# Two blocks of a transformer on one core: norms by token, loads and dots in another order, rotation on VectorE

## What is computed

```
x = first_block(x, ...)
    h = rms_norm(x, norm1_g);  proj = h @ w_in
    ya = rglru_group(...)      # y = gelu(gate) * scan;  rms_norm over 256 channels
    yb = fox_group(...)        # softmax attention, 8 heads of 64; rms_norm over 512
    yc = rwkv7_group(...)      # o = (o - mean) * rsqrt(var + GN_EPS) per head of 64,
                               # ... * ln_g + ln_b, plus a bonus, times g
    x = x + concat(ya, yb, yc) @ w_out
    x = x + hier_moe(rms_norm(x, norm2_g), ...)
return second_block(x, c, positions, ...)
    for l in range(2):
        mod = silu(c) @ w_ada[l] + b_ada[l]      # 6 x 1024 numbers per layer
        h = rms_norm(x, norm1) * (1 + sc1) + sh1;  proj = h @ w_in[l]
        # retention (q and k rotated by the position), spatial gating, pooling,
        # branch and output products, then a feed-forward of width 4096
```

## Time and profile before

| | |
|---|---|
| median of 3 runs (lowest to highest) | 2919.86 us (2915.3 to 2921.07) |
| the profiled execution: time, span | 2918.53 us, 2916.7 us |
| mean granted TensorE clock | 0.957 |
| busy: PE, DVE, ACT, POOL | 2737.2, 1510.6, 1115.2, 904.5 us |
| instructions | 34325 |

### The profile page before, as it was taken

One profiled execution on the slowest core, in us unless ns is written; L12 is line 12 of the kernel. 1 busy time (PEld: TensorE's weight loads), 2 busy tenths in 40 slices (PEclk: granted clock), 3 DMA queues, 4 the chain that ended last, 5 costly groups with the idle time before them and its releaser, 6 DMA issues.

```text
span 2916.7 us, 34325 instructions
## 1 busy us (share of the span) xinstructions
PE 2737.2 (94%) x13246; PEld 2262.8 (78%) x13246; DVE 1510.6 (52%) x1661; ACT 1115.2 (38%) x1283; POOL 904.5 (31%) x200
## 2 busy tenths in 40 slices
PE   6999887999989999997989999899999989899997
PEld 4787565988769898886868888688988867788886
DVE  6755566599943420344246766733212351466666
ACT  3423363577732443234332332324342343333222
POOL 2211002000023244343434444232343434344443
PEclk8999688799999999998999999899999999999999
DMA  7110017299812122222234444321222222244443
GB/s 274 58 44 23 30 44 295 110 365 366 313 69 76 55 97 100 87 101 94 87 120 162 186 165 152 106 87 58 90 92 92 96 94 87 107 155 179 169 152 130
DMA packets 65321, 376.66 MB, mean 129 GB/s; under 512 B 7729, under 2 KB 8753, under 8 KB 29873
## 3 DMA queue, kind: packets, MB, share of 16 engines
q1 hardware_dynamic: 63040, 368.58, 34.5%
q10 hardware_dynamic: 2160, 6.42, 0.6%
HBM read 372.86 MB, written 2.10 MB: 129 GB/s over the span
## 4 chain that ended last, share of the span: by engine, by line
PE 75%; DVE 4%; issue 3%; POOL 1%; ACT 1%; ACTq 0%; DVEq 0%; POOLq 0%
PE pd L240 18%; PE pd L241 18%; PE pd L242 18%; PE pd L260 2%; PE pd L261 2%; PE pd L259 2%; PE pd L1765 2%; PE pd L1763 2%; PE pd L1764 2%; POOL sb_w_lo L218 1%; DVE sb_ada_held L369 1%; PE pd L1790 1%; PE pd L1792 1%; PE pd L1791 1%; PE pd L1721 1%
## 5 line engine op out<-in xcount | busy, mean ns | idle before, releaser
L218 POOL TENSOR_TENSOR sb_w_lo<-sb_raw,sb_w_hi 128x2048 fp32r<-128x2048 f32 x189 | 890.8, 4714 | 1818.0 <-ACT sb_w_hi L209 1818.0
L240 PE MATMUL pd<-sb_h_hi,sb_w_hi 128*128 128x512 f32 x1696 | 676.1, 399 | 53.3 <-DVE sb_h_lo L337 25.6
L241 PE MATMUL pd<-sb_h_lo,sb_w_hi 128*128 128x512 f32 x1696 | 666.2, 393 | 0.0
L242 PE MATMUL pd<-sb_h_hi,sb_w_lo 128*128 128x512 f32 x1696 | 665.2, 392 | 0.0
L209 ACT CAST sb_w_hi<-sb_raw 128x2048 fp32r<-128x2048 f32 x189 | 361.3, 1912 | 316.6 <-PE pd L242 314.5
L240 PEld LDWEIGHTS pd<-sb_h_hi,sb_w_hi 128*128 128x128 f32 x1696 | 322.3, 190 | 132.2 <-DVE sb_h_lo L337 29.7
L240 PE MATMUL pd<-sb_y_hi,sb_w_hi 128*128 128x512 f32 x960 | 377.0, 393 | 20.9 <-issue 17.1
L241 PE MATMUL pd<-sb_y_lo,sb_w_hi 128*128 128x512 f32 x960 | 376.3, 392 | 0.0
L242 PE MATMUL pd<-sb_y_hi,sb_w_lo 128*128 128x512 f32 x960 | 376.0, 392 | 0.0
L241 PEld LDWEIGHTS pd<-sb_h_lo,sb_w_hi 128*128 128x128 f32 x1696 | 322.4, 190 | 67.8 <-issue 2.2
L242 PEld LDWEIGHTS pd<-sb_h_hi,sb_w_lo 128*128 128x128 f32 x1696 | 322.1, 190 | 67.8
(11 more groups left out here) (504 smaller groups left out, 3927.8 us busy)
## 6 DMA issues: line engine op xcount, KB each, us to landing
sb_raw<-in_slabs SPq DMA_DIRECT2D x189, 1024.0 KB, 4.8
sb_V<-in_ada SPq DMA_DIRECT2D x64, 512.0 KB, 6.1
sb_V<-in_moe SPq DMA_DIRECT2D x28, 1024.0 KB, 7.0
sb_QK<-in_moe SPq DMA_DIRECT2D x28, 1024.0 KB, 7.1
sb_raw<-in_moe SPq DMA_DIRECT2D x28, 1024.0 KB, 7.1
sb_QK<-in_ada SPq DMA_DIRECT2D x32, 512.0 KB, 6.5
sb_ada_held<-in_ada SPq DMA_DIRECT2D x30, 512.0 KB, 5.4
sb_M<-in_ada SPq DMA_DIRECT2D x12, 512.0 KB, 15.2
```

The lines of the kernel that those rows point to most:

```text
L218: pool.tensor_tensor(w_lo[j][:], raw[j][:], w_hi[j][:].bitcast(F32), ALU.subtract).then_inc(w_lo_ready[j], 1)
L240: pe.matmul(out, w_hi[j][:, cols], hi[:, k], start=(k == 0), stop=False)
L241: pe.matmul(out, w_hi[j][:, cols], lo[:, k], start=False, stop=False)
L242: last = pe.matmul(out, w_lo[j][:, cols], hi[:, k], start=False, stop=(k == KT - 1))
```

## The change

Four parts. (1) At the start: ScalarE loads the table of the root first and applies Silu to c only behind the cast of slab 1; slab 1 is loaded right behind slab 0; the six dots ahead of the first reciprocal are gone, so that the start has twelve instead of eighteen. (2) Attention: the sums of the two norms are made by token. The tile is the stationary operand and one or two columns of ones the moving one, which gives 4 + 16 columns with the tokens on the partitions; root and reciprocal act on these 128 x 20 numbers, and products of a broadcast column with the identity spread them again over the channels. This stage has twenty dots, one behind each of the units 5 to 24; three blocks of queries are turned at the end instead of two. Some banks of PSUM are given out otherwise, so that `pd[3]` is free earlier, and unit 0 waits for all eight normalised tiles. (3) w_out: 6, 6 and 4 dots. (4) Rotation: VectorE multiplies each half of the tile by the sine and writes it to the other half, in two instructions of 64 partitions; the sine has the other sign, and the swap matmuls go.

The diff, cut to its core and moved left by eight columns; the small hunks left out only rename or number banks and semaphores:

```diff
@@ -55,8 +55,8 @@
 PAIRS = LAYERS_AT + LAYERS * LAYER_PAIRS
 ADA_COLS = 48
 ADA_RING = 6
-ADA_BEFORE, ADA_FIRST, ADA_FOX, ADA_HELD = 6, 18, 10, 4
-ADA_LATE = (7, 8, 5)
+ADA_FIRST, ADA_FOX, ADA_HELD = 12, 20, 4
+ADA_LATE = (6, 6, 4)

 CH = 64
...
@@ -496,15 +495,15 @@
         sp.dma_start(xT[:, 2 * n:2 * n + 2], t["x"][:, 2 * n:2 * n + 2]).then_inc(x_loaded[n], 16)
     sp.dma_start(ones[:], t["ones"]).then_inc(vec_loaded, 16)
     sp.dma_start(vec[:, 0:V1_COLS], t["vec1"]).then_inc(vec_loaded, 16)
-    sp.dma_start(raw[0][:], t["slabs"][0]).then_inc(raw_loaded[0], 16)
+    for j in range(2):
+        sp.dma_start(raw[j][:], t["slabs"][j]).then_inc(raw_loaded[j], 16)
     sp.dma_start(c_row_first, t["c_row"].partition_broadcast(P)).then_inc(c_row_first_loaded, 16)
-    for n in range(ADA_BEFORE):
+    for n in range(6):
         sp.dma_start(ada_first[n], t["ada"][n]).then_inc(ada_first_loaded[n // 3], 16)
-    sp.dma_start(raw[1][:], t["slabs"][1]).then_inc(raw_loaded[1], 16)
     sp.dma_start(c1[:], t["c1"]).then_inc(c_loaded, 16)
     sp.dma_start(blk[:], t["blk"]).then_inc(c_loaded, 16)
     sp.dma_start(ident[:], t["ident"]).then_inc(c_loaded, 16)
-    for n in range(ADA_BEFORE, ADA_FIRST):
+    for n in range(6, ADA_FIRST):
         sp.dma_start(ada_first[n], t["ada"][n]).then_inc(ada_first_loaded[n // 3], 16)
     for m in range(1, 3):
...
@@ -769,20 +768,38 @@
     qk_spreads(6)
     qk_spreads(7)

-    def lru_means():
-        pe.wait_ge(qk_norm, 8)
+    def token_sums():
+        pe.wait_ge(lru_sq, 2)
+        pe.wait_ge(ln_sq, 2)
         for j in range(2):
-            pe.wait_ge(lru_sq, j + 1)
-            last = pe.matmul(pd[3][:], ones[:], lru_sqr[:, j], start=(j == 0), stop=(j == 1))
+            for b in range(TB):
+                pe.matmul(pd[3][:, b:b + 1], lru_sqr[:, j, b * P:(b + 1) * P], ones[:, 0:1],
+                          start=(j == 0 and b == 0), stop=False, skip_group_check=True)
+        for j in range(2):
+            for b in range(TB):
+                at = 4 + 8 * j + 2 * b
+                last = pe.matmul(pd[3][:, at:at + 2], ln_v[:, j, b * P:(b + 1) * P], blk[:, 0:P:CH],
+                                 start=False, stop=(j == 1 and b == TB - 1), skip_group_check=True)
         last.then_inc(lru_sum, 1)

-    def ln_variance(j):
+    def spread_lru():
+        pe.wait_ge(sums_out, 2)
+        for b in range(TB):
+            last = pe.matmul(pd[3][:, b * P:(b + 1) * P], small[:, 64 + b:65 + b].to_broadcast([P, P]),
+                             ident[:], start=True, stop=True)
+        last.then_inc(lru_spread, 1)
+
+    def spread_ln(j):
         if j == 0:
-            pe.wait_ge(lru_total, 1)
+            pe.wait_ge(y_lru, 2)
         else:
-            pe.wait_ge(ln_out, 1)
-        pe.wait_ge(ln_sq, j + 1)
-        pe.matmul(pd[3][:], blk[:], ln_v[:, j], start=True, stop=True).then_inc(ln_var, 1)
+            pe.wait_ge(y_rwkv, 1)
+        for b in range(TB):
+            for g in range(2):
+                at = 68 + 8 * j + 2 * b + g
+                last = pe.matmul(pd[3][g * CH:(g + 1) * CH, b * P:(b + 1) * P],
+                                 small[:, at:at + 1].to_broadcast([P, CH]), ident[:], start=True, stop=True)
+        last.then_inc(ln_spread, 1)

     def scores(n):
...
@@ -832,33 +849,31 @@
     for n in range(len(UNITS) + 3):
         if n < len(UNITS):
             scores(n)
-        if n == 5:
-            lru_means()
-        if n in (7, 9):
-            ln_variance((n - 7) // 2)
+        if n == 7:
+            token_sums()
+        if n == 15:
+            spread_lru()
+        if n in (17, 19):
+            spread_ln((n - 17) // 2)
         if 2 <= n < len(UNITS) + 2:
             turn(n - 2)
         if n >= 3:
             weigh(n - 3)
-        if n == 25:
-            pe.wait_ge(ln_out, 2)
+        if n == 21:
+            pe.wait_ge(y_rwkv, 2)
             turn_block(0, pd[3])
-        if n == 27:
...
-            pe.wait_ge(y_fox, 1)
-            turn_block(1, pd[3])
-    pe.wait_ge(y_fox, 2)
-    turn_block(2, pd[3])
+    pe.wait_ge(y_fox, 1)
     pe.wait_ge(sc_exp, len(UNITS))
-    turn_block(3, pd[2])
+    for i in range(1, TB):
+        turn_block(i, pd[4 - i])

 @block.scalar
 def _(act):
     a = steps["scalar"] = Steps(act, scalar_steps)
+    act.preload_act_table(ACT.Sqrt)
     for n in range(4):
         act.wait_ge(x_loaded[n], 16)
         norm_squares(act, M[:, 0:8], [n])
-    act.wait_ge(c_row_first_loaded, 16)
-    act.activation(c_row_first, c_row_first, ACT.Silu).then_inc(c_row_first_ready, 1)
     split(act, 0, 0)
     norm_scalar(act, 0, M[:, 0:8], first=4)
     act.wait_ge(vec_loaded, 32)
...
@@ -873,8 +888,11 @@
     for m in range(2):
         for j in range(2):
             split_next(act, m, j)
+            n = 2 * m + j
+            if n == 0:
+                act.wait_ge(c_row_first_loaded, 16)
+                act.activation(c_row_first, c_row_first, ACT.Silu).then_inc(c_row_first_ready, 1)
             act.wait_ge(slab_done[j], m + 1)
-            n = 2 * m + j
             act.copy(A[:, 2 * n], pd[2 * j][:])
             if n < 3:
...
@@ -1095,26 +1113,16 @@
             for j in range(2):
                 act.wait_ge(lru_val, j + 1)
                 act.activation(lru_sqr[:, j], lh[:, j], ACT.Square).then_inc(lru_sq, 1)
-        if n == 6:
-            act.wait_ge(lru_sum, 1)
-            act.copy(lru_rstd, pd[3][:]).then_inc(lru_total, 1)
-        if n in (8, 10):
-            j = (n - 8) // 2
-            act.wait_ge(ln_var, j + 1)
-            act.copy(ln_v[:, j], pd[3][:]).then_inc(ln_out, 1)
-        if n == 11:
-            act.wait_ge(lru_total, 1)
-            act.activation(lru_rstd, lru_rstd, ACT.Sqrt, bias=EPS, scale=1.0 / 256).then_inc(lru_root, 1)
-            for j in range(2):
-                act.wait_ge(ln_out, j + 1)
-                act.activation(ln_v[:, j], ln_v[:, j], ACT.Sqrt, bias=GN_EPS,
-                               scale=1.0 / CH).then_inc(ln_root, 1)
-        if n == 20:
-            block_roots(0)
+        if n == 12:
+            block_roots(0, 1)
+            act.wait_ge(sums_out, 1)
+            act.activation(small[:, 64:68], small[:, 64:68], ACT.Sqrt, bias=EPS, scale=1.0 / 256)
+            act.activation(small[:, 68:84], small[:, 68:84], ACT.Sqrt, bias=GN_EPS,
+                           scale=1.0 / CH).then_inc(ln_root, 1)
         if n == 22:
             act.wait_ge(y_lru, 2)
             split_next(act, IN1_PAIRS - 1, 1)
-    block_roots(2)
+    block_roots(1, 3)

 @block.vector
...
@@ -1128,9 +1136,6 @@
             dve.tensor_tensor_reduce(ada_first[n], ada_first[n], c_row_first, 1.0, 0.0, ALU.mult, ALU.add,
                                      mod[:, n:n + 1]).then_inc(ada_used, 1)

-    dve.wait_ge(c_row_first_ready, 1)
-    ada_begin(0, ADA_BEFORE)
-    dve.wait_ge(ada_used, ADA_BEFORE)
     norm_vector(dve, v, 0, M[:, 0:8], lambda k: v1("norm1", k))
     v(dve.tensor_scalar(small[:, 24:26], vec[:, V1["ka"]], -1.0, 1.0, ALU.mult, ALU.add))

@@ -1138,7 +1143,9 @@

     for n in range(7):
         if n % 2 == 0:
-            ada_begin(*((6, 2), (8, 4), (12, 4), (16, 2))[n // 2])
+            if n == 0:
+                dve.wait_ge(c_row_first_ready, 1)
+            ada_begin(*((0, 2), (2, 4), (6, 4), (10, 2))[n // 2])
         if n % 2 == 0:
             dve.wait_ge(slab_out[(n // 2) % 2], n // 4 + 1)
...
@@ -1365,16 +1372,17 @@
           ln_cen, j + 1)

     def rwkv_out(j):
-        v(dve.scalar_tensor_tensor(ln_c[:, j], ln_c[:, j], v1("ln_g", j), ln_v[:, j], ALU.mult, ALU.mult))
+        dve.wait_ge(ln_spread, j + 1)
+        v(dve.scalar_tensor_tensor(ln_c[:, j], ln_c[:, j], v1("ln_g", j), pd[3][:], ALU.mult, ALU.mult))
         v(dve.scalar_tensor_tensor(ln_c[:, j], ln_c[:, j], v1("ln_b", j), bonus[:, j], ALU.add, ALU.add))
...
@@ -1409,37 +1417,32 @@
         if n == 3:
             lru_scan(1)
             lru_times(1)
-        if n == 13:
-            dve.wait_ge(lru_root, 1)
-            v(dve.reciprocal(lru_rstd, lru_rstd))
+        if n == 9:
+            dve.wait_ge(lru_sum, 1)
+            v(dve.tensor_copy(small[:, 64:84], pd[3][:, 0:20]), sums_out, 1)
         if n == 14:
+            block_inverses(0, 1)
+            dve.wait_ge(ln_root, 1)
+            v(dve.reciprocal(small[:, 64:84], small[:, 64:84]), sums_out, 2)
+            scale_block(0)
+        if n == 16:
+            dve.wait_ge(lru_spread, 1)
             for j in range(2):
-                v(dve.scalar_tensor_tensor(Y[:, j], lh[:, j], v1("lru_norm", j), lru_rstd, ALU.mult,
+                v(dve.scalar_tensor_tensor(Y[:, j], lh[:, j], v1("lru_norm", j), pd[3][:], ALU.mult,
                                            ALU.mult), y_lru, j + 1)
-        if n in (15, 17):
-            j = (n - 15) // 2
-            dve.wait_ge(ln_root, j + 1)
-            v(dve.reciprocal(ln_v[:, j], ln_v[:, j]))
-        if n in (16, 18):
-            rwkv_out((n - 16) // 2)
-        if 5 <= n <= 11 or 19 <= n <= 21:
```

(49 more changed lines are left out.)

45 lines of the change are left out of this document (22 added, 23 removed).

## The result

The changed kernel takes 2894.89 us, median of four runs (2891.22 to 2898.71), against 2920.47 (2915.3 to 2921.22): a ratio of 0.9919, 95% interval 0.9905 to 0.9933. Measured again later (e9) it was 2892.6 against 2919.19, ratio 0.9917 (0.9901 to 0.9933). The forecast was 2894.0. The profiled execution of the change took 2891.22 us with a span of 2889.3, so 27.4 us of span less than before, where the sum said 24.5. It was the shortest of its four executions; the medians are 25.6 us apart. One of the five executions of e11 took 7087 us, which nothing here explains; it is in no ratio.

A forecast was written before the change was run, and what follows sets the result against it. The prediction took TensorE, 75% of the span, as the bound, with waits that it sits out. Terms -7.6 + 0 - 3.9 - 13.0 = -24.5 us, from the profiled 2918.53 us, gave 2894.0 us, range 2885 to 2906.

The forecast's parts named there:

- Start, -7.6: Start: second weight slab 8.8 us earlier, less one dot of 1.2 us ahead of the last token shift; -7.6 us.
- Attention, 0: Attention stage: norms by token and ten added dots taken to balance, 0 us, the middle of the bounds.
- -6.3 and +5.9: Attention bounds: -6.3 us if idle VectorE absorbs dots and matmuls hide, +5.9 if everything added is on the path.
- Behind w_out, -3.9: Behind w_out: four fewer dots bring VectorE's last addition forward, cutting TensorE's 5.13 us wait; -3.9 us, bounds -4.5 and -2.5.
- rival A: Attention: dots lengthen each unit and spreads stop TensorE, +5.9 us, 2899.9 us in all; chance 0.12.
- Rotation, -13.0: Retention projections: four batches of swap matmuls go, 13.7 us, less 0.7 for held remainders; -13.0 us.
- the 0.35 that I took off: Rotation: first remainder held by half of one 0.69 us operation in each layer, +0.7 us in all.
- B, the port: Projections: rotation operations hold POOL at eight remainders a layer and TensorE feels each; 11 us given back, 2905.0; chance 0.07.
- C: Start: dots or slab loads catch up with TensorE, only 2 us of gain remain, 2899.6 us; chance 0.05.
- D: Attention: twenty dots wait for loads through a ring of four buffers, +27 us, slower than before; chance 0.03.
- E: Rotation: TensorE waits for the eighth rotated tile instead, so nothing is gained, 2907.0 us; chance 0.02.

The follow-up runs named there:

- e11: Changed kernel with w_out's second cast at unit 27, attention dots in units 5 to 26 without 16 and 18, two start dots later, an added ScalarE wait: 2890.53 us.
- e10: Changed kernel with each half-height product of the rotation done twice in both layers: 2895.95 us, ratio 0.9916.
- e1: Kernel before with the rotation by VectorE as the only edit: 2905.82 us, ratio 0.9955.
- e2: Kernel before with the norms by token as the only edit, its ten attention dots now in units 5 to 14: 2915.08 us, ratio 0.9985.
- e4: Changed kernel with the start as before, so fourteen dots in the attention stage, units 5 to 18: 2897.62 us, ratio 0.9924.
- e3: Changed kernel with group norm and LRU norm at full width as before, dots still in units 5 to 24: 2907.57 us, ratio 0.9956.
- e6: Changed kernel with 7, 8, 5 dots behind w_out as before and sixteen in attention, units 5 to 20: 2896.64 us, ratio 0.9925.
- e8: Changed kernel with w_out's second cast behind the last roots, attention dots in units 5 to 27 without 16, 18, 20, two start dots later: 2891.41 us.
- e13: e11 with w_out's second cast at unit 21 and dots in units 5 to 27 without 22 to 24: 2888.63 us, ratio 0.9891.

## Why the prediction was right

**Start, -7.6: measured -7.4** at the last token shift (77.30 against 84.71 us), the place that the sum named. Of the 9.0 us at the second slab 1.6 are lost on VectorE up to there: it waits 4.11 us for the Silu and the first dot is held (3.23 us). I had taken off one dot of 1.2 us that would no longer fit, so the size was right and the path another. The -7.3 at the first exponential is partly luck. By 125 us only 5.8 are left: from the last token shift to there the change takes 47.9 us at a granted clock of 0.89 (e9 too, and e10 49.5 at 0.86), where before, e1, e2 and e4, with the old start, all take 46.3 at 0.93. Then come the 3.1 us in which the clock happened to be higher, and 1.7 are lost again ahead of the exponential. Against e4, which has the old start and the same clock from 145 to 165 us, the start brings 5.7 us to the attention stage; e10, whose clock there is that of the kernel before, has a lead of only 2.4 us over it. I had not asked what becomes of the lead between the start and the attention stage, nor what the moved dots cost (e4), which is a matter of the next step.

**Attention, 0: measured -0.4** (and between 0 and +0.9 in e9 and e10), right in size, by a reason that was only half right and with a good share of luck. I took the middle of -6.3 and +5.9 "since the small matmuls fall in units where VectorE's step is the longer one, but the dots fall there too". The runs show two parts that cancel: the norms by token, -7.0 us with ten dots, and ten more dots, +6.6. The dots do not cost evenly: the first four cost nothing that shows, and of the last six's 7.2 us the hold of one by w_out's remainder is 3.8. The norms are worth more the fuller VectorE is, 12.8 us with twenty dots, which is why e3 came out at 2907.57 where I had expected 2900 to 2904. The spreads were mis-sized to the safe side: sixteen half-height ones took 1.09 twice, 2.2 us in all instead of the 3.5 that 0.22 each makes; the sixteen token sums took 3.5 us in one place, as priced, and VectorE waited 5.22 us there.

**Behind w_out, -3.9: measured -4.3** by the wait (5.13 to 0.82), near the bound that I set, and 1.8 us more that stood in no term: the four matmuls behind the wait no longer run at the lower clock (3.78 to 1.98 us; e6 brings both back). This is the largest part of the 2.9 us between sum and span. I had used that argument, that TensorE's breaks cost twice, for rival A only.

**Rotation, -13.0: measured -13.1 alone (e1) and -13.3 in the change.** TensorE's wait for the first remainder grew by 0.09 us in layer 0, not by the 0.35 that I took off.

**The rivals.** B, the port, came as a mechanism but at other places. In the rotation the remainders were held by at most 0.5 us and VectorE's operations by 4.2 to 4.4 each (4.93 us for one of 0.69), four times in layer 0 alone, and TensorE felt none of it. The Trainium skill (SBUF — State Buffer, section "SBUF: two separate sides") says that whichever of the two starts first holds the shared ports for its whole instruction; the trace agrees (4.93 and 5.02 us), and it is VectorE that pays most, as POOL's instruction is the long one. I had looked for the price at TensorE's remainders, and at VectorE only behind w_out. It was paid in attention (5.02 us for a dot), a place where I took one operation more per unit as the cost. The trace of before had it to see: the dot of 4.59 us at 18.23, token shifts of 4.97, 4.91 and 4.98 us at 51.13, 64.44 and 75.55, and two operations of 4.51 us in the rotation of layer 0. A did not come: the stage's granted clock rose from 0.83 to 0.89. C did not come by its own mechanism, dots or slabs that catch up, though e10 keeps only 2.4 us of the start's lead, by the clock; in e8 a held product did it. D is excluded: loads of dots land after 4.6 us, had 5.4, and the dots start within 0.2 us of the operation ahead of them. E is excluded with at least 18 us to spare (e10).

## What to carry to other kernels

A step that VectorE and POOL meet in is priced at VectorE's side too: an operation on two SBUF tiles that starts just behind a long POOL instruction ends only after it, so place such operations, or the POOL instruction, where the loss hides. A stage as long as before can hide a gain and a loss of equal size, and undoing one part at a time shows them. A wait removed on TensorE can also return the full clock to the matmuls behind it (here 1.8 us beside 4.3). And before a lead at a landmark is put down to a change, the same landmark is worth reading in a second execution: here 3 us of it came from a stretch in which both programs do the same.

## What was not expected of the hardware

- What the remainder holds depends on the operation. An operation with a single input in SBUF can be held as well: VectorE's `tensor_scalar` of 128x512 at 829.44 us of the change (L2399), 0.02 us behind a remainder, took 4.83 us, where the same form took 0.43 at 836.48. Beside the remainder of attention (413.13 to 418.55 us) the reduction of unit 24, from PSUM, took its usual 0.29 us at 414.10 and a reciprocal of one column its 0.16 at 414.42; the dot at 414.62 took 5.02. In e13 a dot that met only the last half microsecond took 1.73.
- Each of the float32 matmuls of the token sums and spreads stands in the trace as two records. One with one or two columns and new weights takes 0.21 to 0.22 us from start to start (the sixteen from 366.15 to 369.64 us), no less than one of 128 columns (0.22, the four from 390.04 to 390.93); one of 128 columns on half the height takes 0.13 (the eight from 395.03 to 396.05).
- An engine that gets ahead can lose all of it: in e8 a single VectorE product that came 4.3 us earlier met a remainder and gave back all that had been gained.
